# Two transformer-like blocks in one kernel: limiting how long the second recurrence's due matmuls run before a piece of weight matmuls

## The reference

```python
h = rms_norm_2(x, attn_norm[i])
z = h @ w_in[0]                                   # 2048 x 4384: pool part, r, k, v, and small ones
...
d = causal_multiscale_pool(z_pool)
pool_out = einsum('btgc,gcd->btgd', d, pool_w[i]) * pool_scale[i]
rwkv_out, v_first = rwkv7_time_mix(...)           # 16 heads of 64; a recurrence over the 256 tokens:
#   sa = S a_t;  S = S * w_t + sa b_t + v_t k_t;  y_t = S r_t
mix = concatenate([pool_out, rwkv_out], axis=-1)
x = x + mix @ w_out[i]                            # 2048 x 2048
h2 = rms_norm_2(x, mlp_norm[i])
x = x + square(relu(h2 @ w_ffn_up[i])) @ w_ffn_down[i]
gate = sigmoid(rms_norm_2(x, ple_norm[i]) @ w_ple_gate[i])
x = x + gate * (p[i] @ w_ple_proj[i])
```

## Time and profile before

| | |
|---|---|
| median of 3 runs | 2891.03 us (2889.33 to 2894.1) |
| the profiled execution | 2893.31 us, of which the span of the trace is 2891.5 us |
| mean granted TensorE clock | 0.988 |
| TensorE matmuls busy | 2822.6 us, 98% of the span |
| TensorE weight loads | 2459.7 us, 85% (beside the matmuls) |
| VectorE, ScalarE busy | 1897.1 us (66%), 1496.5 us (52%) |
| chain that ended last | TensorE 85%, VectorE 7%, ScalarE 4% |
| transfers | 485.45 MB, 168 GB/s over the span |

### The profile page before, as it was taken

How to read it: one execution, slowest core, us unless ns; L and a number is a source line. 1 busy time by engine, 2 the same in 40 slices (tenths; PEclk the granted TensorE clock), 3 DMA queues, 4 the chain that set the end, 5 groups by cost and what they waited for, 6 DMA issues and landing times.

```text
span 2891.5 us, 40482 instructions
## 1 busy us (share of the span) xinstructions
PE 2822.6 (98%) x16244; PEld 2459.7 (85%) x16244; DVE 1897.1 (66%) x2237; ACT 1496.5 (52%) x2026; POOL 155.2 (5%) x131
## 2 busy tenths in 40 slices
PE   8998999999999999999999999999999999999998
PEld 7988987888888888888888998887788888888886
DVE  6467766455568777777777667655666666566665
ACT  5456655444455545554556556554644444444464
POOL 1010011000000000000000022021000000000000
PEclk9999999999999999999999999979999999999999
DMA  6544522665666666656666522412456566665654
GB/s 215 190 147 143 176 80 91 197 196 183 188 199 187 193 193 190 190 183 193 192 189 182 188 89 81 132 45 87 146 194 190 182 198 191 192 190 189 192 172 160
DMA packets 133819, 485.45 MB, mean 168 GB/s; under 512 B 14944, under 2 KB 16352, under 8 KB 133120
## 3 DMA queue, kind: packets, MB, share of 16 engines
q1 hardware_dynamic: 133632, 482.87, 52.9%
HBM read 480.71 MB, written 2.10 MB: 167 GB/s over the span
## 4 chain that ended last, share of the span: by engine, by line
PE 85%; DVE 7%; ACT 4%; issue 2%; DMA 1%; POOL 0%; DVEq 0%; ACTq 0%; SPq 0%; POOLq 0%
PE psm L187 77%; PE psb L187 7%; ACT ar L203 2%; DVE ar L225 2%; PE psb L190 1%; DVE ar L215 1%; DVE slo L215 1%; ACT shi L203 1%; DMA raw<-in_w_in 1%; DVE x L215 0%; DVE ar L229 0%; DVE gs L225 0%; ACT hf L203 0%; ACT gs L203 0%; ACT L203 0%
## 5 line engine op out<-in xcount | busy, mean ns | idle before, releaser
L215 DVE TENSOR_TENSOR slo<-raw,shi 128x1024 fp32r<-128x1024 f32 (+1 forms) x901 | 1117.7, 1245 | 624.4 <-ACT shi L203 622.3
L203 ACT ACTIVATE shi<-raw 128x1024 fp32r<-128x1024 f32 (+1 forms) x901 | 946.7, 1054 | 1040.3 <-PE psm L187 845.3
L187 PE MATMUL psm<-shi,gs 128*128 128x512 f32 x2016 | 635.0, 391 | 0.2 <-DVE slo L215 0.2
L187 PE MATMUL psm<-gs,shi 128*128 128x256 f32 (+2 forms) x2592 | 550.9, 330 | 11.7 <-DVE slo L215 10.9
L187 PE MATMUL psm<-hs,shi 128*128 128x512 f32 (+1 forms) x2528 | 562.2, 346 | 0.0
L187 PEld LDWEIGHTS psm<-gs,shi 128*128 128x128 f32 (+1 forms) x2592 | 431.0, 191 | 51.5 <-DVE slo L215 11.6
L187 PEld LDWEIGHTS psm<-hs,shi 128*128 128x128 f32 x2528 | 426.7, 189 | 47.8 <-issue 1.4
L187 PE MATMUL psm<-shi,hs 128*128 128x512 f32 x1408 | 453.2, 396 | 10.0 <-DVE slo L215 5.4
L187 PEld LDWEIGHTS psm<-shi,gs 128*128 128x128 f32 x2016 | 378.8, 188 | 80.2 <-issue 1.9
L187 PE MATMUL psm<-slo,gs 128*128 128x512 f32 x1008 | 392.6, 390 | 0.0
L187 PE MATMUL psm<-gs,slo 128*128 128x256 f32 (+1 forms) x1808 | 366.3, 284 | 0.0
(11 more groups left out here) (184 smaller groups left out, 1715.6 us busy)
## 6 DMA issues: line engine op xcount, KB each, us to landing
raw<-in_w_in SPq DMA_DIRECT2D x240, 512.0 KB, 3.7
raw<-in_w_up SPq DMA_DIRECT2D x176, 512.0 KB, 4.1
raw<-in_w_ffn_up SPq DMA_DIRECT2D x128, 512.0 KB, 4.2
raw<-in_w_ffn_down SPq DMA_DIRECT2D x128, 512.0 KB, 4.2
raw<-in_w_down SPq DMA_DIRECT2D x88, 512.0 KB, 3.8
raw<-in_w_out SPq DMA_DIRECT2D x64, 512.0 KB, 4.2
raw<-in_w_ple_gate SPq DMA_DIRECT2D x32, 512.0 KB, 4.2
raw<-in_w_branch_b SPq DMA_DIRECT2D x16, 512.0 KB, 3.6
```

Source lines behind the costliest of these rows:

```text
L187: return self.issued(self.eng and self.eng.matmul(out, lhs, rhs, start=start, stop=stop, skip_group_check=True), cost)
L203: return self.issued(self.eng and self.eng.activation(out, in_, fn, scale=scale, **kw), cost)
L215: return self.issued(self.eng and self.eng.tensor_tensor(out, a, b, op), self.cost(out))
```

## The change

`ready` gets a limit while the second recurrence is planned. Once it has issued steps up to more than 1.0 us of the planner's TensorE clock past its start (or past the time that it was called for, where that is later), it returns, though steps are still due. Then comes the next piece of weight matmuls, and `ready` is called again. The list `mixing` turns this on when pairs 0 to 2 are put into their lanes, and off before the group `fup` is reached. `until` is not limited. No instruction is added or removed, and no number is computed in another way.

```diff
             def ready(until=0.0):
+
+                stop = max(until, pe.t + 1.0)
                 while ws := [w for w in open_lanes() if due(w) <= max(pe.t, until)]:
+                    if mixing and pe.t > stop:
+                        break
                     lane_step(min(ws, key=due))
...
                 if h == 0:
                     until((dve_step, ("scale", 3)))
                     advance(("open_pairs", 0))
+                    mixing.append(True)
                     lanes[0].append(pairs_of(0))
...
                 for f in range(4):
                     group(("out2b", h, f))
+            mixing.clear()
             advance("open_fup")
```

More of the change, by code:

```diff
@@ L2596, in plan_order @@
             order, lanes, want, first = [], [[], [], [], []], [[], [], [], []], []
-            low, building, pairs, whole = [], [0], [], []
+            low, building, pairs, whole, mixing = [], [0], [], [], []
             def advance(name):
```

## The result

The changed kernel takes 2911.69 us (median of 4 runs, 2909.38 to 2914.02), against 2890.18 us for the kernel before in 4 runs. The ratio is 1.0067, with a 95% interval from 1.0051 to 1.0084: slower. The forecast of 2896.6 us had the sign of its likeliest case right, but the time lies outside the range (2885 to 2907), at the time that I gave to the rival *Much slower*. The profiled execution took 2909.38 us, with a span of 2907.6, so it is 16.1 us longer in the trace than that of before.

A forecast was written before the change was run, and what follows sets the result against it. It took the kernel as bound by TensorE, with matmuls busy for 98% of the span. Terms +15.4 - 10 - 1.3 + 1.5 = +5.6 us on the profiled 2893.3 gave 2898.9, less 2.3 over the median: 2896.6 us, range 2885 to 2907.

The forecast's parts named there:

- Much slower: Rival, pairs 4 to 6: a quarter of pieces doesn't keep the clock up, nothing regained; +18.9, 2910 us; chance 14%.
- Changes between pieces and steps: Pairs 0 to 3: more frequent switches between weights and pairs cost nothing; if not, some 20 more would be 2 us.
- The gain: mixed steps keep the clock up: Pairs 4 to 6: pieces among the steps regain 60% of the 16.7 us lost in two half-clock stretches; -10 us.
- Pair 7 loses its cover: End of pair 7: pieces run out fourteen steps early, so the bare chain takes 27 us against 11.6; +15.4 us.
- Faster: Rival: the clock also holds in pair 7's lonely end and the rest is regained; -10.5, 2880.5 us; chance 13%.
- The wait in `G` of pair 4: Two pieces of 0.69 us between the parts of `G` shorten TensorE's 2.0 us wait for VectorE; -1.3 us.
- Pairs 0 to 3: First stage, split more finely and ending later, but covered by `rkv`; +1.5 us, with ends -1 and +3.

The follow-up runs named there:

- e4: Changed kernel with the limit on only from the last `G` of pair 6; 2909.91 us, ratio 1.0055 to the kernel before.
- e10: Kernel before plus the limit from the end of `rkv` to the end of pair 7, lane of pair 4, then pair 7, going first; 2888.39 us, ratio 0.9995.
- e7: Kernel before plus the limit from the end of `rkv` to pair 6's last `G`, lane of pair 4, then pair 7, going first; 2871.59 us, ratio 0.9929.
- e5: Changed kernel with some 45 useless matmuls put between the steps of pair 7's bare end; 2903.66 us, ratio 1.0039 to the kernel before.
- e6: e1 with a limit of nothing in place of 1 us, so a weight piece behind every step; 2897.39 us, ratio 1.0013 to the kernel before.
- e11: e7 with a limit of 2.5 us in place of 1 us; 2890.84 us, ratio 0.9994 to the kernel before.
- e9: Kernel before with no limit, only the rule that the lane of pair 4, then pair 7, goes first; 2888.61 us, ratio 0.9991.
- e12: e7 with the limit ended once the first products of pairs 4 to 6 are issued; 2884.58 us, ratio 0.9972 to the kernel before.
- e8: Changed kernel in full, with the lane of pair 4, then pair 7, going first; 2893.89 us, ratio 1.0001 to the kernel before.
- e13: e7 with the limit begun only once the first products of pairs 4 to 6 are issued; 2877.54 us, ratio 0.9947 to the kernel before.
- e1: Changed kernel with the limit on only for pairs 0 to 3, off once `rkv` is done; 2900.11 us, ratio 1.0021 to the kernel before.

## Why the prediction was wrong

Two steps failed above all: the changes between pieces and steps, set at nothing, and "The gain: mixed steps keep the clock up".

**Pair 7 loses its cover (+15.4).** Right in mechanism, and in size: 27.46 us from `X` to the restart where I took 27, and +15.8. The order of the instructions said where the pieces run out. e4, which has this alone, costs 1.0055, and e10 against e7 19 us. But the size is right in part by luck, as e5 shows. At full clock the end takes 23.1 us, where I had 19.8, and the lowered clock costs 4.3 or a little more, where I had 7.9. The first doubling takes 3.8 us (2049.03 to 2052.82) in place of 2.5, since `R` waits 0.96 us for ScalarE. The clock fell only at 2054.0, 5 us after `X`. And some of e5's filling is in the way.

**Changes between pieces and steps (0).** The largest miss: 4.3 us, by the ledger above. I took 0.69 us for a piece that before stood among the pair's steps and took 0.74. And my argument, that a group of small matmuls is 0.11 us shorter ahead of a piece and so pays for the slower first weight matmul, was read from steps with 128 rows and doesn't carry over to `G`, ahead of which the last weight matmul of a piece is slower too. e6 seems to speak against a price: 56 more changes for pairs 0 to 3 cost nothing measurable. No run sets the price for pairs 4 to 7 apart from cover and clock, so this rests on the timelines.

**The clock regained (-10).** The step "The gain: mixed steps keep the clock up" counted both half-clock stretches as caused by unmixed runs. The traces give about 6.7 us. The two stretches behave differently. In the first products the pieces do help. In the seven kernels without a piece behind each of the three products (e11 has two together) the clock fell there in each profiled execution, for 10 to 17 us; in the eight with one it held in six and fell in two. Once it has fallen, pieces don't bring it back at once: in the kernel before, weight pieces run at 0.50 from 1886.82 until 1891.5. The second stretch went with something else: in the eleven profiled kernels with a wait of 1.49 us or more in `G` of pair 4, the clock fell right at it or within some 2 us, mixed or not; in the four with less than 0.8 us it held in three, and fell for 3.5 us in e10. How long it stays down isn't told by the wait: 3 and 6.5 us in e9 and e12, 17 to 24 us in the others. No run takes away the wait and nothing else, so that it causes the fall is likely and not shown. I had noted in *Faster* that the fall followed 2.0 us of waiting, and used it against that rival only, not against my own term.

The Trainium skill ("TensorE: Matmul & The Clock Gate", "HAM oscillation — how this bites in real kernels") puts such a fall down to idle gaps. For the second stretch the traces agree in that a wait stands ahead of it every time, though one of 1.49 to 2.57 us is shorter than the gaps of that section's own kernel. For the first they don't: TensorE was busy for all of the 6.60 us ahead of the fall and the 10.00 us at 0.50.

**The wait in `G` of pair 4 (-1.3).** Wrong: it stayed, at 2.3 us. I took two pieces for cover, but the wait isn't for a fixed time, and only one of the two stands ahead of it. The next part of `G` needs a bank of `psb` that VectorE gives back, and VectorE waits for ScalarE. The timeline of all engines in the changed kernel:

```profile
1901.96 0.48 PE L187 MATMUL psm<-shi,hs 128*128 128x512 f32 x1
...
1902.84 2.05 PE L187 MATMUL psb<-ar 64*128 64x128 f32 x16
...
1903.72 1.04 ACT L203 ACTIVATE shi<-raw 128x1024 fp32r<-128x1024 f32 x1
...
1904.66 0.82 ACT L203 ACTIVATE hf<-hf,ar 128x128 f32<-128x128 f32 x2
1904.82 0.50 PE L187 MATMUL psm<-shi,hs 128*128 128x512 f32 x1
...
1905.38 0.40 PE L187 MATMUL psm<-shi,hs 128*128 128x512 f32 x1
1905.52 0.65 ACT L203 ACTIVATE hf<-hf 128x128 f32<-128x128 f32 x2
...
1907.12 1.06 ACT L203 ACTIVATE ar<-psb 128x256 f32<-128x256 f32 x3
1907.59 0.42 DVE L215 TENSOR_TENSOR ar<-psb,ar 128x256 f32<-128x256 f32 x1 [1.03 <-ACT ar L203]
...
1908.07 0.58 PE L187 MATMUL psb<-ar 64*128 64x128 f32 x1 [2.29 <-DVE ar L215]
```

and of ScalarE in the kernel before:

```profile
1906.11 1.04 ACT L203 ACTIVATE shi<-raw 128x1024 fp32r<-128x1024 f32 x1
1907.06 1.04 ACT L203 ACTIVATE ar<-psb 128x256 f32<-128x256 f32 x3
```

In both kernels ScalarE has the split of a weight tile and steps of another pair (`hf`) ahead of pair 4's copy, and comes to it at the same time, 1907.06 and 1907.12. `G` started 1.1 us earlier in the changed kernel (1902.84, against 1903.92 before), and the one piece of 0.9 us behind its first half only made up for that. Once pair 4 goes first (e7, e8, e10, e13) and pieces stand there, the wait is gone or under 0.8 us.

**Pairs 0 to 3 (+1.5).** Within its ends by the trace (+2.4). The timed runs of e1 say more: 21 parts in 10,000, 6 us (2.9 to 9.3), over my end of +3. But its products of pairs 4 to 6, with the order of before, were at 0.50 for 3.5 us longer than in the kernel before, so not all of this is the pairs' own.

**The sum.** My terms came to +5.6. With the measured ones, +15.8 - 6.7 + 0.4 + 2.4 + 4.3 = +16.2. Of the miss of 10.6 us, 4.3 are the cost that I set at nothing, 3.3 the clock, 1.7 the waits, 0.9 pairs 0 to 3 and 0.4 the cover. The forecast of the time was off by 15.1 us; the other 4.6 are that I took off 2.3 for the profiled execution of before, which lies over its median, and that of the changed kernel lies 2.3 under its own. The rival *Much slower* gave the right time for a wrong reason: the clock wasn't lost in all of the stage.

## What to carry to other kernels

A chain that ends a stage needs its cover at its end. Filler work that is put in evenly from the start is gone when the longest chain is alone: here 19 us lay between a limit that stopped at `G` and one that went on (e7, e10). Ask of each wait what its releaser is queued behind before putting work in front of it. Price the filler where it will stand: a piece of 0.69 us in a run of pieces was 0.88 alone ahead of `G`. And where a fall of the clock follows a wait, the wait is the thing to take away: with pair 4 first and pieces only up to `G`, the kernel ran at 0.9929 (0.9914 to 0.9944) of the time before, the best of all here.

## What the runs showed of the hardware

The clock can fall while TensorE is busy without a gap. In the first products (float32, most of them with 64 or 32 rows) it was at 0.50 in nine profiled kernels with the engine busy throughout, and busy but for 0.04 us at most in the 5.5 us ahead of the fall. In e7 and e12 it fell there although a piece of 128-row weight matmuls of about 0.9 us stood behind each product of about 3.1 us, the order that held 1.00 in six other kernels. The windows of e7_lead_to_g:

```profile
1881.00:1898.00 17.00, 17.00 (x34) 8.47 (x33) 9.90 (x19) 8.71 (x21) 5.71 (x7) 0.51 0.10 34
1898.00:2059.00 161.00, 157.58 (x964) 131.75 (x963) 106.57 (x166) 93.53 (x186) 21.05 (x30) 1.00 0.29 94
```

So one execution doesn't tell what the clock does there. Those of e7 had mean clocks from 0.992, the profiled one at 2879.04 us, to 0.996 at 2868.62 us. The 17 us at half clock are worth 8.5 us, nearly the 7.5 us by which the profiled execution lies over the median of the six. That the others held the clock there is a conclusion from this, and was not seen.
